# Hybrid HGRN2 + DSA + NSA decoder step, two layers on one core: weight ring padded to 48 entries, small weights, gate exponentials and "flat" products moved

## What is computed

```python
h = _rms(x, norm_g)
z = h @ w_in                      # 5,728 + 3*1024 columns, split into all inputs below
# A: HGRN2, 4 heads of 128x128 state, gated linear recurrence
# B: DSA: lightning indexer scores, top 64 (prompt) or 256 (decode) keys, attention
# C: NSA: compressed, selected and window attention, three sigmoid gates per head
gb  = sigmoid(nbg.reshape(B, L, NSA_HEADS, 3))
o_c = gb[..., 0:1] * o_cmp + gb[..., 1:2] * o_sel + gb[..., 2:3] * o_w
ys = jnp.stack([y_a, y_b, y_c], axis=2)           # each times silu of its own gate
gates = jax.nn.sigmoid(jnp.stack([ma, mb, mc], axis=2))
m = jnp.sum(gates * jnp.einsum('blnc,ncd->blnd', ys, w_branch), axis=2)
y = x + m @ w_out
```

## Time and profile before

| | us |
|---|---|
| median of three runs | 1180.84 (1180.57 to 1185.91) |
| the profiled execution, its own time | 1183.94 |
| its span from the first to the last instruction | 1182.3 |
| TensorE busy (matmuls) | 1092.9 (92%) |
| VectorE (DVE) busy | 595.9 (50%) |
| ScalarE (ACT) busy | 425.9 (36%) |
| GpSimd (POOL) busy | 200.9 (17%) |
| mean granted TensorE clock | 0.967 of full |

### The profile page before, as it was taken

One profiled execution on the slowest core, in us unless ns is written; L12 is line 12 of the kernel. 1 busy time (PEld: TensorE's weight loads), 2 busy tenths in 40 slices (PEclk: granted clock), 3 DMA queues, 4 the chain that ended last, 5 costly groups with the idle time before them and its releaser, 6 DMA issues.

```text
span 1182.3 us, 20776 instructions
## 1 busy us (share of the span) xinstructions
PE 1092.9 (92%) x7574; PEld 887.1 (75%) x7574; DVE 595.9 (50%) x1427; ACT 425.9 (36%) x873; POOL 200.9 (17%) x361
## 2 busy tenths in 40 slices
PE   9999998999897799999789999989988978999998
PEld 7887777876585687788568887778766757778887
DVE  3103378878566775214111033788785667742231
ACT  2133532246432675320011335322554326752200
POOL 0200040011022346300020000300111233471000
PEclk9999999999998899999899999999999979999999
DMA  6654358545363689955244643585554547898542
GB/s 179 179 124 125 96 176 248 126 120 159 109 187 92 200 245 268 269 168 148 74 106 142 148 120 113 167 243 123 134 148 127 167 133 220 240 275 261 152 142 73
DMA packets 242723, 192.89 MB, mean 163 GB/s; under 512 B 117822, under 2 KB 224350, under 8 KB 241342
## 3 DMA queue, kind: packets, MB, share of 16 engines
q1 hardware_dynamic: 227358, 140.38, 43.4%
q0 software_dynamic: 15264, 51.19, 13.3%
HBM read 179.10 MB, written 20.80 MB: 169 GB/s over the span
## 4 chain that ended last, share of the span: by engine, by line
PE 74%; DVE 11%; ACT 5%; DVEq 3%; issue 3%; SPq 2%; DMA 2%; ACTq 1%
PE ps L853 21%; PE ps L1006 12%; PE ps L1350 7%; PE ps L1368 5%; PE ps L1230 4%; PE ps L1214 4%; DVE arena L2157 2%; PE ps L1029 2%; PE ps L1254 2%; PE ps L1140 2%; DVE arena L2162 1%; ACT arena L1393 1%; PE ps L1321 1%; SPq L541 1%; PE ps L896 1%
## 5 line engine op out<-in xcount | busy, mean ns | idle before, releaser
L853 PE MATMUL ps<-hT,slab 128*128 128x264 f32 (+1 forms) x1280 | 295.8, 389 | 2.2 <-DMA slab<-in_w_in_dram 2.2
L1393 ACT ACTIVATE arena<-ps 64x256 f32<-64x256 f32 (+17 forms) x348 | 184.7, 552 | 270.4 <-PE ps L1360 73.7
L853 PEld LDWEIGHTS ps<-hT,slab 128*128 128x128 f32 (+1 forms) x1280 | 241.4, 191 | 45.3 <-DMA slab<-in_w_in_dram 2.6
L1006 PE MATMUL ps<-hT,slab 128*128 128x264 f32 x768 | 187.6, 402 | 2.8 <-DVEq L2133 2.8
L1006 PEld LDWEIGHTS ps<-hT,slab 128*128 128x128 f32 x768 | 148.7, 197 | 36.9 <-issue 6.8
L554 POOL DMA_DIRECT2D arena<-in_cache_kv_dram x64 | 34.5, 539 | 397.0 <-PE ps L950 237.6
L1350 PE MATMUL ps<-Y,slab 128*128 128x264 f32 x384 | 85.8, 386 | 0.0
L1350 PEld LDWEIGHTS ps<-Y,slab 128*128 128x128 f32 x384 | 73.0, 190 | 12.5
L1230 PE MATMUL ps<-arena,w 128*128 128x128 f32 x512 | 73.4, 291 | 7.8 <-ACT arena L1393 5.6
L2157 DVE COPY arena<-ps 64x256 f32<-64x256 f32 x96 | 60.7, 633 | 34.2 <-PE ps L1254 33.2
L1230 PEld LDWEIGHTS ps<-arena,w 128*128 128x128 f32 x512 | 65.9, 202 | 12.7 <-DVE arena L2162 6.7
(11 more groups left out here) (383 smaller groups left out, 1438.6 us busy)
## 6 DMA issues: line engine op xcount, KB each, us to landing
slab<-in_w_in_dram SPq DMA_DIRECT2D x48, 1024.0 KB, 5.8
slab<-in_w_in_dram SPq DMA_DIRECT2D x80, 256.0 KB, 3.9
arena<-in_cache_kv_dram SPq DMA_DIRECT2D x64, 192.0 KB, 4.4
arena<-in_cache_kv_dram POOLq DMA_DIRECT2D x64, 192.0 KB, 4.4
arena<-in_cache_kv_dram POOLq DMA_DIRECT2D x64, 128.0 KB, 6.4
arena<-in_cache_kv_dram SPq DMA_DIRECT2D x64, 128.0 KB, 6.2
slab<-in_w_branch_dram SPq DMA_DIRECT2D x16, 512.0 KB, 6.0
slab<-in_w_out_dram SPq DMA_DIRECT2D x8, 1024.0 KB, 4.9
```

The source lines that it names most:

```text
L853: last = mm(ps[0:job[3], n % 2, 0:LT], v[:, k, job[2]:job[2] + job[3]], hT[:, k, :], start=(k == 0), stop=(k == KD - 1))
L1006: last = mm(ps[:, bank, 0:LT], v[:, k, (d % 2) * 128:(d % 2) * 128 + 128], hT[:, k, :], start=(k == 0), stop=(k == KD - 1))
L1393: return A(out, in_, ACT.Copy, scale=scale)
```

## The change

1. Two entries that carry nothing, pad0 ahead of m03 and pad1 ahead of m12, bring `STREAM` to 48 entries. Where the entry three places earlier is a pad, `send` waits for the one six places earlier. iq0 of layer 1 now shares its slot with o1, iq1 with o2, ikw with o3; m03 waits for m01, m10 for m02, m12 for m10.
2. SP issues the small loads of the next layer ahead of b10, behind the two reloads of spilled gate values.
3. ACT's exponentials "nb" come right behind "e", and DVE's addition and reciprocal ahead of the sort. Of the four copies of the compressed output DVE keeps two; ACT makes the other two (a new step `cp_a` "ev"), for which TensorE and DVE gain a wait.
4. TensorE's "flat" products come behind "a diag".

```diff
--- before.py
+++ after.py
@@ -103,12 +103,15 @@
 SLAB_OF = {s[0]: s for s in SLABS}
 STREAM = ([n for n in FRONT + BACK + GATES if n in SLAB_OF] + [s[0] for s in GATE_SLABS] + [s[0] for s in OUT_SLABS])
 STREAM.insert(STREAM.index("m21"), "qr")
+PADS = ("pad0", "pad1")
+for _n, _next in zip(PADS, ("m03", "m12")):
+    STREAM.insert(STREAM.index(_next), _n)
 NSLOT = 3
 
 
 def slab_dmas(name):
 
-    if name == "qr":
+    if name == "qr" or name in PADS:
         return 0
     if name in SLAB_OF:
         return len(SLAB_OF[name][1]) * (2 if name[:2] in PAIRS else 1)
@@ -450,7 +453,7 @@
         cp_p = Steps("cp_p", ["h 0", "h 1", "out 0", "out 1", "s", "t", "o"] + [f"gb {c}" for c in range(3)])
         cp_v = Steps("cp_v", ["sum 0", "sum 1", "s", "n", "nb", "ev"] + [f"gb {c}" for c in range(3)]
                      + ["prompt done"])
-        cp_a = Steps("cp_a", ["hb 0", "hb 1", "hid 0", "hid 1", "out 0", "out 1", "e", "t", "nb"])
+        cp_a = Steps("cp_a", ["hb 0", "hb 1", "hid 0", "hid 1", "out 0", "out 1", "e", "nb", "t", "ev"])
         pg_p = Steps("pg_p", sum([[f"T {u}"] + [f"s {u // 4 - 1}"] * (u >= 4 and u % 4 == 1) for u in range(NU)], []) + [f"s {NS - 1}"])
         pg_a = Steps("pg_a", [f"C {u}" for u in range(NU)])
         pg_v = Steps("pg_v", sum([[f"C {u}", f"D {u}"] + [f"W {u // 4}"] * (u % 4 == 3) for u in range(NU)], []))
@@ -617,6 +620,8 @@
                     if at_ >= NSLOT:
 
                         old = STREAM[at_ - NSLOT]
+                        if old in PADS:
+                            old = STREAM[at_ - 2 * NSLOT]
                         if old in SLAB_OF:
                             sp.wait_ge(proj_ready, l * NJOB + LAST_JOB[old])
                         elif old == "qr":
@@ -700,10 +705,10 @@
                     sp.wait_ge(spill_out[a], l * 16 + 16)
                     sp.wait_ge(dx_p.sem, dx_p(l, "x 0"))
                     sp.dma_start(sig[a], spill[a]).then_inc(back_in[a], 16)
+                if l + 1 < DEPTH:
+                    small_loads(l + 1)
                 for name in STREAM[STREAM.index("b10"):]:
                     send(name)
-                if l + 1 < DEPTH:
-                    small_loads(l + 1)
             for t in range(2):
                 sp.wait_ge(y_a.sem, y_a(0, f"y {t}"))
                 sp.wait_ge(y_v.sem, y_v(0, f"y {t}"))
@@ -982,11 +987,6 @@
                 project("hi1", 0)
                 key_scores(3)
                 project("hi1", 1)
-                pe.wait_ge(sidx_a.sem, sidx_a(l, "relu"))
-                for q in range(4):
-                    h2 = halves[q // 2]
-                    last = mm(ps[eight[q], 7, 0:NQ], iwS[h2], RI[h2, (q % 2) * NQ:(q % 2) * NQ + NQ], start=True, stop=True)
-                last.then_inc(sidx_p.sem, sidx_p.mark("flat"))
                 gates = iter(GATE_JOBS)
                 mixes = iter(range(NMIX))
 
@@ -1015,6 +1015,11 @@
                     for h in range(4):
                         last = mm(ps[:, 2 + t, h * 128:h * 128 + 128], kT[:, h, t * 128:t * 128 + 128], Zq[:, h, t * 128:t * 128 + 128], start=True, stop=True)
                 last.then_inc(hg_p.sem, hg_p.mark("a diag"))
+                pe.wait_ge(sidx_a.sem, sidx_a(l, "relu"))
+                for q in range(4):
+                    h2 = halves[q // 2]
+                    last = mm(ps[eight[q], 7, 0:NQ], iwS[h2], RI[h2, (q % 2) * NQ:(q % 2) * NQ + NQ], start=True, stop=True)
+                last.then_inc(sidx_p.sem, sidx_p.mark("flat"))
                 for i in range(8):
                     pe.wait_ge(hg_v.sem, hg_v(l, f"m {i}"))
                     b = 4 if i % 2 == 0 else 2
@@ -1198,6 +1203,7 @@
                     last.then_inc(cp_p.sem, cp_p.mark(f"gb {c}"))
                     if c == 0:
                         pe.wait_ge(cp_v.sem, cp_v(l, "ev"))
+                        pe.wait_ge(cp_a.sem, cp_a(l, "ev"))
                     mix(5 + c)
 
 
@@ -1632,14 +1638,19 @@
                 take(2)
                 act.wait_ge(cp_v.sem, cp_v(l, "s"))
                 A(SC, SC, ACT.Exp).then_inc(cp_a.sem, cp_a.mark("e"))
+                for q in range(4):
+                    last = A(nbs[32 * q:32 * q + 24, :], Z[32:56, Z_IW, :], ACT.Exp, scale=-1.0)
+                last.then_inc(cp_a.sem, cp_a.mark("nb"))
                 take(3)
                 take(2)
                 act.wait_ge(cp_p.sem, cp_p(l, "t"))
                 copy(PTC[0:NCP].rearrange("p h t -> p (h t)").rearrange("p (b c) -> p b c", b=4), ps[0:NCP, 0:4, :]).then_inc(cp_a.sem, cp_a.mark("t"))
-                for q in range(4):
-                    last = A(nbs[32 * q:32 * q + 24, :], Z[32:56, Z_IW, :], ACT.Exp, scale=-1.0)
-                last.then_inc(cp_a.sem, cp_a.mark("nb"))
-                for bank in (7, 5, 6, 7):
+                take(7)
+                act.wait_ge(cp_p.sem, cp_p(l, "o"))
+                for g, r in enumerate(halves):
+                    last = copy(OC[r, 0, :, 128:256], ps[r, 5 + 2 * g, :].rearrange("p (j t) -> p j t", j=4))
+                last.then_inc(cp_a.sem, cp_a.mark("ev"))
+                for bank in (5, 6, 7):
                     take(bank)
 
 
@@ -2119,20 +2130,21 @@
                 ve.drain()
                 TT(SC, SC, K("cmp_mul").rearrange("p (t c) -> p t c", t=2).unsqueeze(2).to_broadcast([128, 2, NH, NCP]), ALU.mult)\
                     .then_inc(cp_v.sem, cp_v.mark("n"))
+                ve.wait_ge(cp_a.sem, cp_a(l, "nb"))
+                TS(nbs[0:120, :], nbs[0:120, :], 1.0, None, ALU.add)
+                ve.drain()
+                nc.vector.reciprocal(nbs[0:120, :], nbs[0:120, :]).then_inc(cp_v.sem, cp_v.mark("nb"))
                 best_of_pairs()
                 sort_pairs()
                 threshold()
-                ve.wait_ge(cp_a.sem, cp_a(l, "nb"))
-                TS(nbs[0:120, :], nbs[0:120, :], 1.0, None, ALU.add)
-                ve.drain()
-                nc.vector.reciprocal(nbs[0:120, :], nbs[0:120, :]).then_inc(cp_v.sem, cp_v.mark("nb"))
                 ve.wait_ge(cp_p.sem, cp_p(l, "o"))
                 for g, r in enumerate(halves):
-                    for t in range(2):
-                        TC(OC[r, 0, :, t * 128:t * 128 + 128], ps[r, 4 + 2 * g + t, :].rearrange("p (j t) -> p j t", j=4))
+                    TC(OC[r, 0, :, 0:128], ps[r, 4 + 2 * g, :].rearrange("p (j t) -> p j t", j=4))
                 ve.drain().then_inc(cp_v.sem, cp_v.mark("ev"))
                 for c in range(3):
                     ve.wait_ge(cp_p.sem, cp_p(l, f"gb {c}"))
+                    if c == 0:
+                        ve.wait_ge(cp_a.sem, cp_a(l, "ev"))
                     TT(OC[:, c], ps[:, 0:4, 0:LP], OC[:, c], ALU.mult)
                     TC(gbs[:, 4 * c:4 * c + 4, :], ps[:, 0:4, seq_cols])
                     ve.drain().then_inc(cp_v.sem, cp_v.mark(f"gb {c}"))
@@ -2166,11 +2178,11 @@
                         nc.vector.transpose(block_keys(s, 1)[:, NPG:NPG + 4, :], kws[s % 2]).then_inc(pg_v.sem, pg_v.mark(f"W {s}"))
                         if s:
                             join(s - 1)
-                    if w == 2:
+                    if w == 6:
                         compared()
-                    if w == 4:
+                    if w == 10:
                         limits()
-                    if w == 6:
+                    if w == 14:
                         dropped_ties()
                 join(NS - 1)
```

More of the change, by code:

```diff
@@ L2121, in _ @@
                     .then_inc(cp_v.sem, cp_v.mark("n"))
-                best_of_pairs()
-                sort_pairs()
-                threshold()
                 ve.wait_ge(cp_a.sem, cp_a(l, "nb"))
@@ L2128, in _ @@
                 nc.vector.reciprocal(nbs[0:120, :], nbs[0:120, :]).then_inc(cp_v.sem, cp_v.mark("nb"))
+                best_of_pairs()
+                sort_pairs()
+                threshold()
                 ve.wait_ge(cp_p.sem, cp_p(l, "o"))
                 for g, r in enumerate(halves):
-                    for t in range(2):
-                        TC(OC[r, 0, :, t * 128:t * 128 + 128], ps[r, 4 + 2 * g + t, :].rearrange("p (j t) -> p j t", j=4))
+                    TC(OC[r, 0, :, 0:128], ps[r, 4 + 2 * g, :].rearrange("p (j t) -> p j t", j=4))
                 ve.drain().then_inc(cp_v.sem, cp_v.mark("ev"))
```

## The result

The changed kernel takes 1163.43 us (median; 1158.76 to 1170.43) against 1180.70 for the kernel before beside it, a ratio of 0.9854 [0.9812, 0.9897]. By the ratio that is a gain of 17.2 us (12.2 to 22.2), where 31.35 was forecast: 14 us are missing. The profiled execution took 1164.59, its span from first to last instruction is 1162.9.

What follows compares the result with a forecast made beforehand. TensorE, busy 92% of the span, was taken as the bound: 16.05 (layer's end) + 6.5 (diagonal) + 12.0 (gates) - 0.9 (port) - 2.3 (clock) = 31.35 us, giving 1149.5 at the median; range 1142.9 to 1160.9.

Steps and rivals of the forecast that it cites:

- a new wait later in the layer as long as those that went: Listed among the signs that would show the forecast wrong; no size or place given.
- Rival 3: Inside the layers, DVE's chain takes the gains back; only the layer's end pays, 16.05 us, 1164.8; chance 0.08.
- End of layer 0: Earlier small weights gain 9.55 us, earlier first slab of the next layer 6.5; together 16.05.
- The pads' 0: Later sending of m03, m10, m12 costs 0; only m12 is close, with 3.4 us of cover per layer.
- rival 2: m12 comes late, sharing DMA engines with page loads; 11.4 us off the gain, 1160.9; chance 0.09.
- rivals 4 and 5: 4: iq0 still follows o3, 1156.0, chance 0.03; 5: m12 far later, slower, about 1187 at 28 us, chance 0.02.
- The diagonal: HGRN2 diagonal, both layers: scores ahead of flat start "a 0" earlier; 6.5 us together.
- The gates: Branch gates, both layers: the mix behind them starts 3.1 us earlier and runs at full clock; 12.0 us together.
- The port: At the gates, POOL's memset holds the threshold's last copies, delaying DVE's copies 0.45 us per layer; 0.9 off.
- Clock: Four stretches inside the layers return to 2.4 GHz; one fall of the four allowed, 2.3 us off.

Runs made afterwards that it cites:

- Experiments 1 and 2: 1: changed kernel with page steps back at w = 2, 4, 6, 1153.56 us; 2: kernel before with them at 6, 10, 14, 1195.47 us.
- experiment 5: Changed kernel with page steps at w = 2, 4, 6 again, 1148.52 us; 2, 4, 8, 1142.46; 4, 8, 12, 1153.30; 2, 4, 14, 1149.80.

## Why the prediction was wrong

**The step that failed** is the one that is missing. The prediction goes through the layer's end, the pads, the diagonal and the gates; it says nothing of the three page steps moved from w = 2, 4, 6 to 6, 10, 14, although they stand in the diff. The list in "The change" leaves them out as well. The moved steps were thus put at nothing, without a reason. Their price could be read from the trace before: `limits()` at 2.34 us against a wait of only 0.16 at 412.46, and `dropped_ties()`, 1.84 us at w = 6, with TensorE's 2.77 behind it at 401.13. One line of the text had named the sign, "a new wait later in the layer as long as those that went"; it was not priced. Experiments 1 and 2 put it at 10.7 and 15.1 us. Without it the forecast's 31.35 meets 27.9 (25.0 to 30.7), just above the interval.

**Rival 3** gave 1164.8 and lies next to the measured 1163.4, by luck. It had the diagonal and the gates taken back by DVE's chain behind them; alone they keep 5.6 and 7.1 us.

**End of layer 0.** Right: 16.05 forecast, 16.1 measured; 6.5 and 9.55 against 7.0 and 9.2. The ten small loads did go into SP's pause (issued from 501.71, the last at about 507, next slab at 513.38).

**The pads' 0.** Right: no wait at mix n = 12, so rival 2 did not occur, nor rivals 4 and 5.

**The diagonal.** 6.5 forecast before clock falls, 5.6 (2.6 to 8.4) measured. In layer 0 "a 0" moved by 3.3, as drawn; in layer 1 the clock fell and 3.46 us for its 16 matmuls gave 1.5 back. Behind the levels the diagonal alone keeps 3.2 us in layer 0 and 1.5 in layer 1.

**The gates.** Right at the place, too large in the whole: 12.0 less 0.9 forecast, 11.7 at the place in the trace, 7.1 (4.8 to 9.4) timed. The copies came out near their prices (ACT's two 1.20 us, as priced; DVE's two 1.39 for 1.26). Why the whole gain is smaller than that at the place stays open.

**The port.** The 0.9 did not appear: DVE's copies start at 351.78, 0.05 after TensorE's "o" ends. The addition takes 1.90 us in both layers of all six profiles of kernels where POOL's memset starts up to 0.1 us ahead of it, and 0.30 in all eight where it was moved away. But the threshold's copies of 8x1, inside the memset of 349.93 to 351.73, lost only 0.24. The Trainium skill (SBUF — State Buffer, section "SBUF: two separate sides") has a lock for the whole instruction, but only against some of DVE's operations; the rows agree for the 120x264 operation and show that the small copies are not held until the memset ends, as the prediction took from it.

**Clock.** One fall of the four was taken; one came (layer 1's diagonal). Others came where none was priced: in both layers the 128 products at L1327, some 10 us behind m22's wait, take 5.35 us instead of 3.68. With the waits for m22 of 2.08 and 1.90 that is 7.3 us of the changed kernel's profile. The fastest kernel of experiment 5 has the same slow products behind nearly the same waits, so the moved steps do not need to be their cause.

## What to carry to other kernels

Go through a diff hunk by hunk and write a price beside each, a moved number too; the one left at no price cost 11 to 15 of 28 us here. An engine that is busy for half the time can have places without any slack: before moving work onto it, read the wait of the bounding engine for the next thing that it makes, and where that is near zero the work costs about its whole length (2.34 us of `limits()`, a wait of 2.54). Where DVE idled 3.7 us in front of the third group and not at all behind it, a step at the first group left a wait of 1.1 us and one at the third of 2.5 to 2.8.

## What the runs showed of the hardware

Identical instructions run at different granted clocks in different executions of one kernel: the attention from the first to the ninth mix took 72.0 or about 74 us in the profiles, in either layer, and no edit explains which. Six executions of one kernel spread over 5 to 14 us, and the same kernel (steps at 2, 4, 6) had medians of 1153.56 and 1148.52 in two groups while the kernel before moved by 1.0. So a difference under 5 us was told only from stages of the traces, or from kernels measured side by side. Nor is the difference of two spans a gain: between the profiled executions it is 12.2 us for the gates alone and 9.4 for the layer's end, where 7.1 and 16.1 were timed.

A slab sent among value loads takes far longer than the median of 5.8 us: m22 was issued at 466.83 in the changed kernel and TensorE went on at 483.04, 16.2 us later. The kernel before sent it at 474.52, came to it 15.4 us later and did not wait. The margin at this place is about nil, and the runs do not tell what fills those 15 us.
